# A fused two-block network on one core: products moved from GpSimd to VectorE, another order of TensorE's products in a triangular inverse, and attention steps with scores two ahead

## What is computed

```python
a = jnp.einsum('bhncd,bhnmd->bhncm', k_beta, k) * decay
m = jnp.where(strict, a, 0.0) + jnp.eye(CHUNK)
rhs = jnp.concatenate([v * beta[..., None], k_beta * jnp.exp(g)[..., None]], axis=-1)
sol = lax.linalg.triangular_solve(m, rhs, left_side=True, lower=True, unit_diagonal=True)
qk = jnp.einsum('bhncd,bhnmd->bhncm', q, k) * decay
# attention, for each branch and head
p = masked_softmax(q @ k.T * scale + bias, mask)
o = p @ v
```

## Time and profile before

| | |
|---|---|
| median of 3 runs | 1862.19 us (1858.97 to 1864.44) |
| profiled execution | 1863.49 us, span 1861.7 us |
| mean granted TensorE clock | 0.952 |
| TensorE busy | 1691.2 us, 91% |
| VectorE / ScalarE / GpSimd busy | 721.5 / 455.0 / 27.0 us |
| inverse of the GDN, tile products to T6 | about 370 to 423 us |
| attention steps | about 793 to 850 us |

### The profile page before, as it was taken

One profiled execution on the slowest core, in us unless ns is written; L12 is line 12 of the kernel. 1 busy time (PEld: TensorE's weight loads), 2 busy tenths in 40 slices (PEclk: granted clock), 3 DMA queues, 4 the chain that ended last, 5 costly groups with the idle time before them and its releaser, 6 DMA issues.

```text
span 1861.7 us, 25291 instructions
## 1 busy us (share of the span) xinstructions
PE 1691.2 (91%) x10496; PEld 1052.9 (57%) x10496; DVE 721.5 (39%) x1143; ACT 455.0 (24%) x727; POOL 27.0 (1%) x25
## 2 busy tenths in 40 slices
PE   8999999779999999999999888988899888987985
PEld 5799989666499989775534333333333333423332
DVE  3655557924365561262322231222312222222236
ACT  1544446431244441053212001010010100101003
POOL 0000000300000000000000000000000000000000
PEclk9999999969999999999899999999999999998998
DMA  9544443303254462115999999999999999999993
GB/s 396 208 192 193 194 178 137 137 4 145 87 232 186 185 264 111 46 46 216 368 428 426 427 428 426 429 429 428 428 427 429 428 428 428 426 427 428 428 427 157
DMA packets 41969, 549.58 MB, mean 295 GB/s; under 512 B 4824, under 2 KB 4984, under 8 KB 8728
## 3 DMA queue, kind: packets, MB, share of 16 engines
q1 hardware_dynamic: 39720, 540.45, 69.7%
q0 software_dynamic: 1872, 6.82, 1.0%
q10 hardware_dynamic: 288, 1.05, 0.1%
HBM read 545.12 MB, written 3.18 MB: 295 GB/s over the span
## 4 chain that ended last, share of the span: by engine, by line
PE 73%; DMA 18%; DVE 4%; ACT 2%; issue 2%; SPq 0%; DVEq 0%
DMA ring<-experts_dram 18%; PE ps L552 6%; PE ps L2332 5%; PE ps L2377 5%; PE ps L2355 5%; PE ps L2416 5%; PE ps L741 3%; PE ps L739 3%; PE ps L740 3%; PE ps L665 3%; PE ps L667 3%; PE ps L666 3%; PE ps L2389 2%; PE ps L1590 2%; PE ps L2469 2%
## 5 line engine op out<-in xcount | busy, mean ns | idle before, releaser
L794 DVE TENSOR_TENSOR ring_split<-ring,ring_split 128x1024 fp32r<-128x1024 f32 x156 | 187.1, 1221 | 127.7 <-ACT ring_split L846 127.6
L2355 PE MATMUL ps<-ring,arena 128*32 128x512 f32 x1152 | 158.1, 699 | 79.4 <-DMA ring<-experts_dram 79.4
L2849 DVE TENSOR_SCALAR arena<-ps 128x512 f32<-128x512 f32 (+1 forms) x38 | 21.5, 565 | 487.9 <-PE ps L2355 195.1
L846 ACT CAST ring_split<-ring 128x1024 fp32r<-128x1024 f32 x156 | 160.6, 1047 | 166.4 <-PE ps L741 93.2
L2377 PE MATMUL ps<-ring,arena 128*128 128x512 f32 x384 | 168.1, 596 | 0.2 <-DMA ring<-experts_dram 0.2
L3155 ACT ACTIVATE arena<-arena 128x512 f32<-128x512 f32 (+1 forms) x38 | 20.2, 530 | 568.9 <-DVE arena L2849 568.9
L2355 PEld LDWEIGHTS ps<-ring,arena 128*32 128x32 f32 x1152 | 41.4, 126 | 185.3 <-issue 181.6
L739 PE MATMUL ps<-arena_split,ring_split 128*128 128x256 f32 x512 | 145.3, 284 | 0.0
L741 PE MATMUL ps<-arena_split,ring_split 128*128 128x256 f32 x512 | 144.8, 283 | 0.0
L740 PE MATMUL ps<-arena_split,ring_split 128*128 128x256 f32 x512 | 144.4, 282 | 0.0
L2377 PEld LDWEIGHTS ps<-ring,arena 128*128 128x128 f32 x384 | 73.3, 191 | 88.7 <-issue 86.8
(11 more groups left out here) (455 smaller groups left out, 2409.1 us busy)
## 6 DMA issues: line engine op xcount, KB each, us to landing
ring<-experts_dram SPq DMA_DIRECT2D x192, 2048.0 KB, 19.6
ring<-weights_dram SPq DMA_DIRECT2D x55, 2048.0 KB, 11.2
row_buf<-rows_dram POOLq DMA_DIRECT2D x13, 512.0 KB, 8.8
ring<-heads_dram SPq DMA_DIRECT2D x4, 1024.0 KB, 4.7
ring<-weights_dram SPq DMA_DIRECT2D x3, 1024.0 KB, 11.4
tab<-tables_dram SPq DMA_DIRECT2D x1, 2160.5 KB, 31.3
tab<-weights_dram SPq DMA_DIRECT2D x1, 1536.0 KB, 26.4
gate_mid<-weights_dram SPq DMA_DIRECT2D x1, 1536.0 KB, 28.5
```

The costliest lines, as they stand in the source:

```text
L794: V.tensor_tensor(low, raw, high, ALU.subtract).then_inc(sem("part_low"), 1)
L846: A.copy(split_buffer(MLP_SPLIT_SLOT, buffer)[0], raw).then_inc(sem("part_high"), 1)
L2355: ins = T.matmul(view(bank(0)[TINY * q:TINY * q + TINY], (2, 256)), xs_of(4 * c + d, j)[:, 0:TINY], w[q // 2][:, d, :, 256 * (q % 2):256 * ...
```

## The change

VectorE takes over GpSimd's product of decay and beta (`decay_beta`, one call per tile) and of q and its norms (`unit_q`, one per half). GpSimd keeps the zeroing of TT, now behind the masks of level 2, and its z product now comes after its two copies. Masks of level 2 are made before the first L, later ones one level ahead. On TensorE the large products are put in another order, so that one lies between any two tile products, with unread matmuls around P5 and T5. In the attention the unread matmuls are dropped, `prob` gets three buffers (at another place in SBUF), scores(n + 2) go ahead of turn(n) and values(n - 1) behind it; ScalarE copies a step's turned probabilities after the next step's exponentials, and VectorE's branch sums and ScalarE's branch copy come later by one position.

```diff
@@ pe_gdn_inverse
             far(0, "KK", k, k)
-            far(1, "KK", k, k)
             P_products(1)
             pe.wait_ge(sem("gdn_qkv"), 6)
+            far(1, "v", v, None)
+            T_products(1)
             pe.wait_ge(*flag("gdn_LT0"))
             far(0, "v", v, None)
-            T_products(1)
-            pe.wait_ge(*flag("gdn_LT1"))
-            far(1, "v", v, None)
             P_products(2)
+            pe.wait_ge(*flag("gdn_VB1"))
+            far(1, "k", k, None)
             T_products(2)
             pe.wait_ge(*flag("gdn_VB0"))
             far(0, "k", k, None)
             P_products(3)
+            pe.wait_ge(*flag("gdn_KBG"))
+            far(1, "KK", k, k)
             T_products(3)
-            pe.wait_ge(*flag("gdn_VB1"))
-            far(1, "k", k, None)
+            pe.wait_ge(*flag("gdn_KD"))
+            pe.wait_ge(*flag("gdn_q1"))
+            far(0, "QK", k, q)
             P_products(4)
-            pe.wait_ge(sem("gdn_unit"), 3)
-            pe.wait_ge(*flag("gdn_KD"))
-            far(0, "QK", k, q)
+            pe.wait_ge(*flag("gdn_LT1"))
+            far(1, "QK", k, q)
             T_products(4)
+            pe_keep_running(ps[:, 0, 256:512], 512)
...
-            pe.wait_ge(*flag("gdn_KBG"))
-            far(1, "QK", k, q)
+            pe_keep_running(ps[:, 1, 256:512], 256)
...
+            pe_keep_running(ps[:, 0, 256:512], 512)
@@ a_gdn_inverse
             copy_P(1)
+            scaled_v(1)
+            copy_P(2)
             scaled_v(0)
-            copy_P(2)
-            scaled_v(1)
+            a.wait_ge(*flag("gdn_k1_psum"))
+            a.wait_ge(*flag("gdn_DB1"))
+            for h in range(HEADS):
+                m = A.activation(KBG[:, h * P:(h + 1) * P], ps[:, 3, h * P:(h + 1) * P], ACT.Copy, scale=bg[:, h, 1:2])
+            m.then_inc(flag_up("gdn_KBG"), 1)
             copy_P(3)
...
             copy_P(4)
-            a.wait_ge(*flag("gdn_k1_psum"))
...
-            m.then_inc(flag_up("gdn_KBG"), 1)
             copy_P(5)
@@ v_gdn_inverse
+            def decay_beta(t):
+                V.tensor_tensor(tile_of(LT, t), tile_of(DEC, t), tile_of(spread_beta, t), ALU.mult).then_inc(flag_up(f"gdn_DB{t}"), 1)
+            def unit_q(half_):
+                blocks = qkvT[:, 4 * half_:4 * half_ + 4, :].rearrange("p a b -> p (a b)")
+                V.tensor_tensor(blocks, blocks, half(spread_q, half_), ALU.mult).then_inc(flag_up(f"gdn_q{half_}"), 1)
...
+            masked(2, 0)
+            masked(2, 1)
+            decay_beta(0)
             whole_L(0)
...
-                if l < NEAR:
-                    masked(l + 1, 0)
-                    masked(l + 1, 1)
                 if l == 1:
+                    decay_beta(1)
+                if l == 2:
+                    v.wait_ge(sem("gdn_rows_kept"), 16 + 5 * 16)
+                    unit_q(0)
+                    unit_q(1)
+                if l < NEAR - 1:
+                    masked(l + 2, 0)
+                    masked(l + 2, 1)
+                if l == 3:
                     whole_L(1)
@@ pool_gdn_inverse
-            G.tensor_tensor(LT, DEC, spread_beta, ALU.mult).then_inc(sem("gdn_pool"), 1)
-            pool.wait_ge(sem("gdn_unit"), 2)
+            pool.wait_ge(*flag("gdn_M2_1"))
             G.memset(TT, 0.0).then_inc(sem("gdn_pool"), 1)
-            G.tensor_tensor(q, q, spread_q, ALU.mult).then_inc(sem("gdn_unit"), 1)
@@ pool_gdn_z
             pool.wait_ge(*flag("gdn_z"))
+            pool.wait_ge(sem("gdn_pool"), 4)
@@ the attention
-        prob = view(slot01[:, 0:1536], (2, 2, COLS))
+        PROBS = 3
+        prob = view(slot23[:, 0:768 * PROBS], (PROBS, 2, COLS))
...
             def turn(n):
-                pe.wait_ge(sem("att_raw"), n + 1)
-                pe_keep_running(ps[:, n % 2, 0:512], 512)
                 pe.wait_ge(sem("att_prob"), n + 1)
...
             for n in range(len(STEPS)):
-                turn(n)
                 if n + 2 < len(STEPS):
                     scores(n + 2)
-                values(n)
+                turn(n)
+                if n >= 1:
+                    values(n - 1)
+            values(len(STEPS) - 1)
@@ v_attention
-                if r == 2 and branch > SEL:
+                if r == 3 and branch > SEL:
                     v_att_branch(v, branch - 1)
@@ a_attention
-                if r == 1 and branch > SEL:
-                    out_of(branch - 1)
...
-                turn(n)
+                if r == 1 and branch > SEL:
+                    out_of(branch - 1)
+                if n >= 1:
+                    turn(n - 1)
+            turn(len(STEPS) - 1)
@@ gpsimd block
+            pool_gdn_middle(pool)
             pool_gdn_z(pool)
-            pool_gdn_middle(pool)
```

More of the change, by code:

```diff
@@ L43 @@
     "tensor": (
[L44 to L49, removed]
+        "gdn_ba_psum", "gdn_rows_psum", "gdn_near0_psum", "gdn_near1_psum", "gdn_KK0_psum",
+        "gdn_P1_0_psum", "gdn_P1_1_psum", "gdn_v1_psum", "gdn_T1_0_psum", "gdn_T1_1_psum", "gdn_v0_psum",
+        "gdn_P2_0_psum", "gdn_P2_1_psum", "gdn_k1_psum", "gdn_T2_0_psum", "gdn_T2_1_psum", "gdn_k0_psum",
+        "gdn_P3_0_psum", "gdn_P3_1_psum", "gdn_KK1_psum", "gdn_T3_0_psum", "gdn_T3_1_psum", "gdn_QK0_psum",
+        "gdn_P4_0_psum", "gdn_P4_1_psum", "gdn_QK1_psum", "gdn_T4_0_psum", "gdn_T4_1_psum",
+        "gdn_P5_0_psum", "gdn_P5_1_psum", "gdn_T5_0_psum", "gdn_T5_1_psum",
         "gdn_P6_0_psum", "gdn_P6_1_psum", "gdn_T6_0_psum", "gdn_T6_1_psum",
@@ L57 @@
         "gdn_ba", "gdn_g_in", "gdn_g", "gdn_bg", "gdn_near_decay", "gdn_near0", "gdn_near1", "gdn_M0_0", "gdn_M0_1",
[L58 to L61, removed]
+        "gdn_TT0_0", "gdn_TT0_1", "gdn_T0_0", "gdn_M1_0", "gdn_T0_1", "gdn_M1_1", "gdn_M2_0", "gdn_M2_1", "gdn_DB0", "gdn_LT0",
+        "gdn_T1_0", "gdn_T1_1", "gdn_TT1_0", "gdn_TT1_1", "gdn_DB1", "gdn_M3_0", "gdn_M3_1",
+        "gdn_T2_0", "gdn_T2_1", "gdn_TT2_0", "gdn_TT2_1", "gdn_q0", "gdn_q1", "gdn_M4_0", "gdn_M4_1",
+        "gdn_T3_0", "gdn_T3_1", "gdn_TT3_0", "gdn_TT3_1", "gdn_LT1",
         "gdn_T4_0", "gdn_T4_1", "gdn_TT4_0", "gdn_TT4_1", "gdn_QKT0",
@@ L1316, in a_gdn_inverse @@
             copy_P(4)
-            a.wait_ge(*flag("gdn_k1_psum"))
-            for h in range(HEADS):
-                m = A.activation(KBG[:, h * P:(h + 1) * P], ps[:, 3, h * P:(h + 1) * P], ACT.Copy, scale=bg[:, h, 1:2])
-            m.then_inc(flag_up("gdn_KBG"), 1)
             copy_P(5)
             a.wait_ge(*flag("gdn_TT4_1"))
-            a.wait_ge(sem("gdn_pool"), 3)
+            a.wait_ge(sem("gdn_pool"), 2)
             for name, blocks in (("low", (2, 3)), ("high", (0, 1))):
@@ L1400, in negated @@
                                        -1.0, None, ALU.mult)
-            v.wait_ge(sem("gdn_pool"), 3)
+            v.wait_ge(sem("gdn_pool"), 2)
             for t in range(TILES):
@@ L1438, in pool_gdn_middle @@
                 from_ = near_T[rows_, :, :].rearrange("p t (h c) -> p t h c", h=HEADS)
-                pool.wait_ge(sem("gdn_pool"), 3 + j)
+                pool.wait_ge(sem("gdn_pool"), 2 + j)
                 G.tensor_copy(to, from_).then_inc(sem("gdn_pool"), 1)
@@ L1574, in build @@
         kcc = m_small[:, 336:352]
-        mx = view(m_small[:, 352:368], (2, 8))
+        mx = view(m_small[:, 488:512], (PROBS, 8))
         f_c, f_abs, f_log = (view(m_small[:, 368 + 16 * n:384 + 16 * n], (HEADS, TILES)) for n in range(3))
@@ L1861, in turn @@
                         at = (3 * half_ + b) * P
-                        m = T.transpose(ps[:, 2, at:at + P], prob[:, n % 2, half_, b * P:(b + 1) * P], ident)
+                        m = T.transpose(ps[:, 2, at:at + P], prob[:, n % PROBS, half_, b * P:(b + 1) * P], ident)
                 m.then_inc(sem("att_probT_psum"), 1)
@@ L1899, in v_attention @@
                 v.wait_ge(sem("att_score_psum"), n + 1)
-                if n >= 2:
-                    v.wait_ge(sem("att_probT_psum"), n - 1)
+                if n >= PROBS:
+                    v.wait_ge(sem("att_probT_psum"), n - PROBS + 1)
                 for half_ in range(2):
                     h = head_of(branch, r, half_)
-                    raw, src = prob[:, n % 2, half_, :], ps[:, n % 2, 512 * half_:512 * half_ + COLS]
+                    raw, src = prob[:, n % PROBS, half_, :], ps[:, n % 2, 512 * half_:512 * half_ + COLS]
                     if branch == FOX:
@@ L1958, in a_attention @@
                     for t, (c0, c1) in enumerate(((0, P), (P, COLS))):
-                        m = A.activation(prob[:, n % 2, half_, c0:c1], prob[:, n % 2, half_, c0:c1], ACT.Exp,
-                                         bias=mx[:, n % 2, 4 + 2 * half_ + t:5 + 2 * half_ + t],
+                        part = prob[:, n % PROBS, half_, c0:c1]
+                        m = A.activation(part, part, ACT.Exp, bias=mx[:, n % PROBS, 4 + 2 * half_ + t:5 + 2 * half_ + t],
                                          scale=1.0 if branch == FOX else 2.0 ** -(h + 1),
```

22 lines of the change are left out of this document (8 added, 14 removed).

## The result

The changed kernel takes 1839.49 us (median of 4 runs, 1838.40 to 1842.47) beside 1861.82 us for the kernel before (4 runs): a ratio of 0.9883, 95% interval 0.9864 to 0.9902, or 22.3 us less. Its profiled execution took 1838.40 us around a span of 1836.6, so the profiled spans differ by 25.1 us.

The account below looks back on a forecast made before the run. Apart from expert-weight transfers, TensorE's chain of work was taken to bound the kernel. Inverse 15.8 us (11.8 + 3.0 - 0.8 + 1.8) plus attention 3.7 gave 19.5 us off, 1843 us in medians, range 1833 to 1857.

Parts of the forecast that it names:

- Part 1: Inverse: with GpSimd's products gone, VectorE's masks and quarters run at normal pace and tile products start earlier, 11.8 us gained.
- I cost them at nothing: Inverse: the decay and q products moved to VectorE, 4.7 us of work, are covered and add no time.
- Part 2: Inverse, first tile product to fifth step's second product: one large product between any two tile products gains 3.0 us.
- I take 3.0: Inverse: assumed time in us of a large product within a code block, between 3.78 at half clock and 1.92 at full.
- Part 3: End of the inverse: five unread matmuls cost 0.8 us and bring 1.8 us by a higher clock.
- Part 4: Attention: shorter steps without unread matmuls gain 7.1 us at equal clock, 3.7 us after clock losses.
- two more falls at 1.7: Attention: without unread matmuls the clock falls two more times, 1.7 us each, taking 3.4 us off the gain.
- A microsecond gained should arrive whole: Whole kernel: both edited stages lie on the chain ahead of the expert stage, so time gained there reaches the end.
- A: Rival: the attention's clock drops and stays down, slower than before, 1870 us; chance 5%.
- B: Rival: the attention gives nothing and only the inverse's 15.8 us are gained, 1846 us; chance 20%.
- D: Rival: weight transfers, not GpSimd, cause VectorE's slow lines in the inverse, 1857 us; chance 4%.
- C: Rival: code blocks at 5.4 us each pace the inverse, the first late beside weight transfers, 1852 us; chance 15%.

Follow-up runs that it names:

- part 1 alone: The kernel before with only GpSimd's decay and q products moved to VectorE and its z product put behind the copies: 1855.59 us, ratio 0.9959.
- z early: The changed kernel with GpSimd's z product moved ahead of the zeroing, beside VectorE's masks: 1839.63 us, ratio 0.9869.
- inverse alone: The changed kernel with the attention section of the kernel before: 1848.93 us, ratio 0.9927.
- every step filled: The changed kernel with two unread matmuls in every attention step from the third on, new order kept: 1839.40 us, ratio 0.9883.
- the kernel before without its filler: The kernel before without the unread matmuls in the attention, old order and two buffers kept: 1862.51 us, ratio 1.0004.
- attention alone: The kernel before with only the new attention section: 1855.04 us, ratio 0.9954.
- weights late: The changed kernel with two transfers of the output stage's weights issued only after the inverse's fourth level: 1836.57 us, ratio 0.9867.
- code shifted: The changed kernel with 32 tiny unread matmuls ahead of the inverse's `near` products: 1835.83 us, ratio 0.9851.
- start filled: The changed kernel with five unread matmuls ahead of the scores of attention step 3: 1836.34 us, ratio 0.9849.

## Why the prediction was right, and where its terms were off

The forecast was 1843, the result 1839.5: 19.5 us expected, 22.3 measured in the medians and 25.1 in the profiled spans. Part 1 is right for its own reason. The others add up to about what was forecast partly by luck.

- **Part 1, 11.8 us: right in place, size and cause.** `near` to tile product lost 12.0 us, and the first tile product came at 358.46 for 358.4 forecast. That GpSimd's product is what slows VectorE is shown by taking it away (part 1 alone) and putting one back (z early). GpSimd's z product ran beside VectorE's PSUM readers at 393.72 without harm, as forecast. "I cost them at nothing" for the moved products held only in the new order: in the old one they cost 1.3 us more of waiting for L.
- **Part 2, 3.0 us: the mechanism right in part, the sum wrong.** It brought 7.4. The failing step is the pacing by blocks, "I take 3.0" for a large product and 5.6, 4.8 and 4.7 us for its blocks. It had nothing for the 3.0 us wait for L that the new order took away, and the clock too low. The traces divide the 7.4 us so: 3.0 is the wait; 2.2 are standstills, 10.8 us in seven pieces before (9.8 in the earlier trace rows and 1.0 on a line beside it) and 8.6 in eight after, where the first grew by 1.5, as it now falls beside the weight transfers, and the others shrank by 3.7; 2.2 is busy time, although the new stretch holds one more K product and six more records of unread matmuls, 3.9 us. That is the clock: it was at 0.50 only from 363 to 377 us and then stayed at 1.00, long before any filler. The closest test of the order is the kernel with part 1 alone beside the one without the unread matmuls of the inverse: from the first tile product to T5 45.7 us at a mean clock of 0.66 against 36.2 at 0.84. Over all profiles the old order took 43.3 to 45.7 us at 0.61 to 0.66, and the new one 35.6 to 38.8 at 0.81 to 0.91, with the weights in their old place. So the order's gain is shown. How much of it is the spacing of the large products and how much the lost wait, no run separates. The Trainium skill, "Runtime: NRT & Kernel Launch", "Instruction fetch mechanics", calls the crossing of a block mostly hidden. The eight standstills and their shift by the added matmuls disagree.
- **Part 3, -0.8 + 1.8 us: not borne out.** 1.9 came from T5 to the output stage and 1.5 behind it, 3.4 for 1.0, since the clock stayed up in this profile. But with the same inverse that stretch took 6.2 to 10.2 us in four profiles (changed kernel, inverse alone, start and every step filled), and in the old order without any filler 6.2 to 8.3. That the 1.9 came out is chance of the clock; what decides it is open.
- **Part 4, 3.7 us:** 5.7 came in the stretch. At an equal clock 10.1 (54.3 us for the old section without a fall, 44.2 for the new) in place of 7.1. The start gave 1.7 for a forecast of 1.5. From step 3 to step 11 it was 8.6 for 7.4 - 1.1, since a step is 2.95 us and not 3.10, the last two 2.44, while one step was held up by 0.7 where 1.1 had been put down for the branch sums. The end cost 0.2, not 0.7. The clock term, "two more falls at 1.7", was one fall of 13.7 us, two steps at 5.5 and one at 3.7. The cost was not shared out in small falls: net of the old section's fall it was 4.4 us here for 3.4 put down, and in other profiles of this attention nothing.
- **Not foreseen:** -2.6 us in the router, where the clock was low for longer than before. That stretch took 56.1 to 59.9 us in ten profiles of the new attention and 56.4 to 57.0 in three of the old. The expert stage behind it took 956.0 to 959.9 us over all profiles, though no edit touches it. "A microsecond gained should arrive whole" holds for the chain, but stretches behind it scatter by as much as some of these edits are worth; in the kernel before without its filler 5.2 us gained came back as 5.5 lost.
- **The rivals.** A and B fell with the attention alone, D with the two tests of part 1. C's premise stands for the first step of code (transfers stretch it), its price did not.

## What to carry to other kernels

An engine whose simple lines take several times their usual duration is to be read beside its neighbour's timeline at the same instants: two GpSimd products handed over and a third put later let TensorE start 12 us sooner, though the moved products were free only in an order that gave them room. Small matmuls in unrolled code paid a standstill per block of instructions here, and the order with large ones between them took 7.4 us less, 3.0 of them a wait that went with it. Before trusting one profile of a stretch whose clock varies, compare it with other profiles of the same code: a gain of 2 us at the end of the inverse lay within what the same code shows. Filler in each step of the attention cost 0.92 us a step and did not keep the clock from falling.

## What was unexpected of the hardware

- **VectorE beside GpSimd looks held rather than slowed:** two masks that take 0.76 us took 5.10 beside a GpSimd product of 4.51, ending with it; two took 8.57 us beside two such products. Operations with a PSUM operand kept their 0.75 us. The Trainium skill, "GPSIMD Engine Reference", "Key points", says that GpSimd shares its SBUF interfaces with VectorE, with contention for instructions with two SBUF inputs. The trace agrees.
- **A step of code stretches under transfers:** 3.46 us at a border beside two weight transfers, 0.95 with them later. The later borders together cost 5.1 and 5.8 us, so only the first was shortened, and the 3.4 us gained up to T5 were lost again at a lower clock in all three profiles with the weights late (T5 to output product 10.7 to 11.2 us).
- **The same code is granted different clocks.** Without filler the clock of the new attention fell for 13.7 us in one profile, for 10.2 in another (z early), for 3.4 in a third (attention alone), and not at all in those without the inverse's filler, with the weights later alone, or with the code shifted. With the start filled it did not fall in three profiles of three. That is suggestive and no more: two of these three also had the weights late, which alone had no fall either.
